# A new issue order in causal dilated attention and the recurrence beside it: key and query projections moved ahead, scores ahead of the turn

## The chip, the cores and the metric

The kernel is one program on one core of a Trainium2 chip. The metric is the device time of one execution in microseconds (us); lower is better. A core has a tensor engine (PE, with its weight loads shown apart as PEld), a vector engine (DVE), a scalar engine (ACT), a GpSimd engine (POOL) and a sync engine (SP) that here only issues DMAs. Each engine runs its own instructions strictly in the order in which they are written, and they meet at semaphores.

## What is computed

One decoder layer over 1024 tokens of width 1024, all in float32:

```
xn = rmsnorm(x); q, k, v, u = split(xn @ w_in)             # 4 x 512 columns
y_a = dilated causal attention(q, k, v) with T5 bias        # 8 heads of 64, three (window, dilation) patterns
y_b = S5(u): 32 groups, 64 complex states each, linear recurrence along the sequence, then GELU and a gate
h = x + [rmsnorm(y_a); rmsnorm(y_b)] @ w_out
h = h + cross attention(h, 256 memory rows)                 # its keys and values are projected early
h = h + mixture of experts(h): 4 of 32, 1024 wide, clamped SwiGLU
out = rmsnorm(h)
```

The three patterns of the dilated attention are handled as one softmax whose bias holds the logarithm of how many patterns include a distance, and minus 1e30 where none does.

## The kernel before

The program is five phases with a barrier of all engines after each. The change is wholly in the first, `phase_abc`: the projections, the set-up of the recurrence, the recurrence itself and the self attention. The later phases (the recurrence's output, the output projection, cross attention, the experts, the last norm) start when all engines have ended the first.

**Two rings of PSUM banks.** Transposes and small products go through `put` (L771), which uses banks 0 to 3 in turn: the product for place g waits until what place g-4 holds has been copied out. The list `plan(...)` (L317 to L344) says in which order the places come and whether ACT or DVE copies each. The wide projections go through `project` (L787), with banks 4 to 7 in turn; one projection product is eight 128-deep matmuls of up to 512 columns. The products are numbered: U (0 to 7), the memory keys (8 to 11), the memory values (12, 13), K (14 to 21), Q (22 to 29), V (30 to 37). The numbers, banks and weights of these are not changed. The weights of the six projections alternate between two buffers of 2 MB, `wa0` and `wa1`: U in 0, memory keys in 1, memory values in 0, K in 1, Q in 0, V in 1.

**The order on PE (L806 to L891).** The three small products for the attention's bias line (L814, one-hot rows times `rel_bias`); x transposed for the first half and U of it; x for the second half and the other U products; transposes for the recurrence's parameters; memory rows transposed, memory keys, memory values; then PE waits for `bt_ok` and `cp_step` 27, which say that the tables `BT` (built by POOL, L1084 to L1088) and `Cp` (built by DVE in `cp_of`, L626, nine steps of three operations over 128x512) are ready; then come the mixer's first products: transposes of `BT` (L855) and products with `U`, whose results DVE and ACT copy into `V`; the products that give `Krow`; the K projection; the products with `M1` (L884); the Q projection; the V projection; and last the attention. POOL starts the recurrence (L1098 to L1107, 128 steps of four dependent operations on `V`) when all of `V` is there. `M1` comes from `Krow` by way of a write to memory and eight loads by SP.

**The order on DVE (L634 to L707).** DVE copies the bias line, scales half of x's transposes, evicts the U products, then does `cp_of(0)`, the memory transposes, and for each memory key product one `cp_of`, the eviction, and one more `cp_of`; then its share of `V`, the K evictions, the `M1` results (32 operations), and the Q evictions.

**The order on SP (L387 to L468).** One queue: it loads the x rows and parameters; with U's products done it loads the weights of unit 2, writes `uT` to memory, waits for that write, issues the eight loads of `U`, and only then waits for the memory keys and loads the K weights, then the Q weights. Later come `Krow` out, `M1` in, the bias tiles 0 and 1, the V weights, and at the end bias tiles 2 and 3.

**The attention (L710 to L765, L893 to L967, L545 to L582).** There are 32 tiles t, each two heads and one block b of 128 queries (b runs from 0 to 7 inside each of four head pairs). For each tile there are these steps:

- `scores(t)` on PE: the near part (L900) and for b of 2 or more the far part (L906), into one of two pairs of banks;
- `maxima(t)` on DVE (L720): adds the bias, negates, and gives the row's extreme, for two heads;
- `exps(t)` on ACT (L557): exponentials and their sums;
- `divide(t)` on DVE (L727, L731): reciprocals of the sums, and the probabilities scaled by them;
- `turn(t)` on PE: transposes of the probabilities, near part (L917) into bank 4 and far part (L925) into bank 5;
- `near(t)` on ACT (L568) and `far(t)` on DVE (L745, L748): copies out of these two banks;
- `values(t)` on PE (L936), and at the end of a head pair `far_values` (L950), the squares on ACT (L573) and `out_of` on DVE (L755).

What the order of issue is, engine by engine, for each t:

```
PE :  turn(t)       scores(t+2)   values(t-1)   [far_values]
DVE:  maxima(t+1)   divide(t)     far(t)        [out_of]
ACT:  exps(t+1)     near(t)                     [squares_of]
```

Of the kernel before, what the change touches and what calls it, by code (L numbers as in the profile page):

```python
# [31 lines left out]
H_A, HD_A = 8, 64  # L32
# [8 lines left out]
T = 8  # L41
J = S // T
# [248 lines left out]
def phase_abc(nc, block, m, a, sem):  # L291
# [23 lines left out]
    banks, at = [], {}  # L315

    def plan(name, who):  # L317
        at[name] = len(banks)
        banks.append(who)

    for n in range(3):
        plan(("line", n), "dve")
    for half in range(2):
        for k in range(KC):
            plan(("x", half, k), "act" if k % 2 == 0 else "dve")
        plan(("rsb", half), "dve")
    plan("prm", "act")
    plan(("c", 0), "act")
# [17 lines left out]
    def t_bank(g):  # L346
        return m.ps[:, g % 4, :]
# [237 lines left out]
    def _(dve):  # L585
        def line_out_(n):
            g = at[("line", n)]
            dve.wait_ge(t_full, g + 1)
            lo, hi = 512 * n, min(512 * n + 512, LINE)
            nc.vector.tensor_copy(m.line[:, lo:hi], t_bank(g)[0:H_A, 0:hi - lo]).then_inc(t_dve, 1)  # L590
# [44 lines left out]
        nc.vector.memset(m.ztile[:], 0.0).then_inc(zero_ok, 1)  # L635
        for n in range(3):
            line_out_(n)
        dve.wait_ge(mix_in, 16)
# [4 lines left out]
        rsb_out(0)  # L643
        u_out_(0)
        for k in range(1, KC, 2):
            x_out(1, k)
# [13 lines left out]
        u_out_(7)  # L660
        cp_of(0)
        dve.wait_ge(gain_in, 16 * 14)
# [4 lines left out]
        for c in range(H_X):  # L667
            i = KM0 + c
            cp_of(1 + 2 * c)
            dve.wait_ge(p_full, i + 1)  # L670
            nc.vector.tensor_copy(m.kmT[:, c, :], p_bank(i)[:, 0:N_MEM]).then_inc(p_dve, 1)
            cp_of(2 + 2 * c)
        for q in range(8):
            g = at[("v", 1, q)]
            dve.wait_ge(t_full, g + 1)
            nc.vector.tensor_copy(m.V[:, 1:J + 1, 1, 4 * q:4 * q + 4], t_bank(g).rearrange("p (g j) -> p j g", g=4)).then_inc(t_dve, 1)

        def head_out(i, dst, s):
# [8 lines left out]
        for n in range(8):  # L687
            c, half = divmod(n, 2)
            head_out(K0 + n, m.kT[:, c, half * 512:(half + 1) * 512], None)
        for q in range(8):  # L690
            g = at[("y", q)]
            dve.wait_ge(t_full, g + 1)
            for n in range(4):
                w = 4 * q + n
                last = nc.vector.scalar_tensor_tensor(out=m.U[:, w, :], in0=m.U[:, w, :], scalar=m.dskip[:, w:w + 1],
                                                      in1=t_bank(g)[:, n * P:(n + 1) * P], op0=ALU.mult, op1=ALU.add)
            last.then_inc(t_dve, 1)
        dve.wait_ge(k_out, 16)
        for n in range(8):
            c, half = divmod(n, 2)  # L700
            head_out(Q0 + n, m.qT[:, c, half * 512:(half + 1) * 512], HD_A ** -0.5)

# [55 lines left out]
        for t in range(N):  # L758
            if t + 1 < N:
                maxima(t + 1)  # L760
            divide(t)
            far(t)
            if t % NB == 0 and t:
                out_of(t // NB - 1)
        out_of(3)  # L765

    @block.tensor
    def _(pe):
        group, product = [0], [0]

        def put(emit):  # L771

            g = group[0]
            if g >= 4:
                t_copied(pe, g - 4)
            emit(t_bank(g)).then_inc(t_full, 1)
            group[0] += 1
# [31 lines left out]

        pe.wait_ge(ones_row, 1)  # L810
        pe.wait_ge(oh_in, 32)
        for n in range(3):
            lo, hi = 512 * n, min(512 * n + 512, LINE)
            put(lambda out: nc.tensor.matmul(out[0:H_A, 0:hi - lo], m.rb[:], m.ohb[:, lo:hi], start=True, stop=True))  # L814
        pe.wait_ge(ident_ok, 3)
# [3 lines left out]
        for k in (6, 7):  # L819
            t_copied(pe, at[("x", 0, k)])  # L820
        by_weights(0, 0, 0)
        x_in_(1)
        by_weights(0, 1, 0)
# [33 lines left out]
        def four(operand, width=P):  # L857
# [5 lines left out]
            put(emit)  # L863

        pe.wait_ge(bt_ok, 1)
        pe.wait_ge(cp_step, 27)
# [9 lines left out]
        for q in range(8):  # L876
            four(lambda n: (m.BT[:, 4 * q + n, P - CH:P], m.Cp[:, 4 * q + n, 0:P]), CH)
        pe.wait_ge(wa_in[3], 16)
        for c in range(4):
            for half in range(2):  # L880
                by_weights(3, c, half)
        pe.wait_ge(m1_in, 16 * T)
        for q in range(8):
            four(lambda n: (m.M1[:, 4 * q + n, :], m.U[:, 4 * q + n, :]))  # L884
        pe.wait_ge(wa_in[4], 16)
        for c in range(4):
            for half in range(2):
                by_weights(4, c, half)
        pe.wait_ge(wa_in[5], 16)
        for b in range(NB):  # L890
# [66 lines left out]
        for i in range(V0 + 4, PROJECTED):  # L957
            p_copied(pe, i)
        for t in range(N + 1):
            if t < N:  # L960
                turn(t)
            if t + 2 < N:
                scores(t + 2)
            if t:
                values(t - 1)
                if t % NB == 0:
                    far_values(t // NB - 1)  # L967
# [1514 lines left out]
```

## Time and profile before

| what | us |
|---|---|
| median of 3 runs | 2673.07 (2672.39 to 2673.39) |
| the profiled execution, its own time | 2668.99 |
| its span in the profile | 2667.3 |
| 84 to 142, from the memory transposes to the mixer's first products | 58 |
| 342 to 494, the attention | 152 |
| 494 to 2667, the later phases | 2173 |

Times in the profile count from the start of the span. "PE busy" counts a pipelined matmul from its start to its modelled end, so the start of one group to the start of the next is the better measure of what it occupies. "idle before" is the time for which the engine did nothing ahead of that instruction, and the arrow names who released it. SPq is SP issuing a DMA: its length is that of the issue, not of the transfer. PEclk is the granted clock of PE, 1.00 for 2.4 GHz and 0.50 for 1.2 GHz.

### The profile page before, as it was taken

The numbers are of one execution on the slowest core, as the hardware profiler recorded it, in microseconds if no ns is written. First come the engines' busy times: TensorE is split into PE (matmuls) and PEld (weight loads), VectorE is DVE, ScalarE is ACT, GpSimd is POOL, SyncE is SP. The second block draws the span as 40 slices with busy tenths as digits, with TensorE's granted clock in tenths as the row PEclk, the third lists the DMA queues.
The fourth block names the chain that finished last, engine by engine and source line by source line (L and its number), as shares of the span: only waits on it lengthen the run. The fifth ranks groups of instructions, "written<-read, shape, count | busy, mean of one in ns | idle before, by whom it ended". The sixth has DMA issues, their size and how long they took to land. (4 is left out here: it accounts for less than half of the span.)

```text
span 2667.3 us, 29283 instructions
## 1 busy us (share of the span) xinstructions
PE 2454.2 (92%) x11352; PEld 1616.8 (61%) x11353; DVE 649.9 (24%) x1537; ACT 367.8 (14%) x824; POOL 422.4 (16%) x992
## 2 busy tenths in 40 slices
PE   8799966899989669999999999999999999999993
PEld 4465434645444257778696696786786786684441
DVE  2522044322243621112121221221221221221111
ACT  3020033201132000101101011011011111011101
POOL 3858810001001010000001001001000001001002
PEclk9899977898999889999999999999999999999996
DMA  8641000520001646776878878878888888889854
GB/s 191 136 66 38 24 15 1 161 77 32 0 1 58 254 143 191 229 244 217 260 253 267 274 252 268 280 261 259 277 270 263 294 285 281 294 291 304 287 181 142
DMA packets 373344, 508.04 MB, mean 190 GB/s; under 512 B 49031, under 2 KB 234631, under 8 KB 373204
## 3 DMA queue, kind: packets, MB, share of 16 engines
q1 hardware_dynamic: 360872, 469.43, 53.6%
q0 software_dynamic: 11008, 35.89, 6.0%
q8 instruction: 91, 1.49, 0.2%
q10 hardware_dynamic: 1324, 0.83, 0.1%
q14 instruction: 49, 0.40, 0.0%
HBM read 469.39 MB, written 38.77 MB: 191 GB/s over the span
## 5 line engine op out<-in xcount | busy, mean ns | idle before, releaser
L2055 PE MATMUL ps<-xT,we 128*128 128x160 f32 (+9 forms) x3584 | 516.4, 307 | 1.4 <-ACT xT L2302 1.4
L2055 PEld LDWEIGHTS ps<-xT,we 128*128 128x128 f32 x3584 | 508.3, 190 | 15.0 <-issue 8.0
L1997 PE MATMUL ps<-we,xT 128*128 128x512 f32 x1152 | 506.8, 594 | 0.0
L1997 PEld LDWEIGHTS ps<-we,xT 128*128 128x128 f32 x1152 | 213.8, 190 | 258.6 <-issue 258.6
L2069 PE MATMUL ps<-actT,we 128*128 128x160 f32 (+9 forms) x1792 | 261.1, 307 | 0.0
L2069 PEld LDWEIGHTS ps<-actT,we 128*128 128x128 f32 x1792 | 253.4, 190 | 5.6 <-DVE outT L2216 2.1
L2021 PE MATMUL ps<-we,actT 128*128 128x512 f32 x576 | 255.1, 596 | 0.7 <-ACT actT L2333 0.7
L1892 POOL DMA_INDIRECT acc_dram<-orow,sx x46 | 70.9, 1542 | 781.0 <-ACT orow L2313 488.2
L2325 ACT ACTIVATE sg<-glu 128x512 f32<-128x512 f32 (+9 forms) x92 | 49.8, 541 | 1041.1 <-DVE glu L2171 550.2
L2021 PEld LDWEIGHTS ps<-we,actT 128*128 128x128 f32 x576 | 106.5, 190 | 135.1 <-issue 134.2
L793 PE MATMUL ps<-xnT,wa 128*128 128x512 f32 x384 | 165.9, 592 | 0.0
L2190 DVE TENSOR_SCALAR glu<-ps,b1s 128x160 f32<-128x160 f32 (+9 forms) x112 | 44.0, 393 | 497.9 <-PE ps L2055 497.9
L1880 POOL DMA_INDIRECT xg<-xn_dram,gx x46 | 50.7, 1101 | 594.1 <-PE ps L1956 585.2
L793 PEld LDWEIGHTS ps<-xnT,wa 128*128 128x128 f32 x384 | 72.6, 190 | 90.1 <-issue 90.1
L286 POOL TENSOR_SCALAR ss<-ss 128x1 f32<-128x1 f32 (+1 forms) x36 | 7.9, 220 | 524.9 <-DVE ss L1315 171.6
L2171 DVE TENSOR_SCALAR glu<-ps 128x512 f32<-128x512 f32 x36 | 24.9, 692 | 270.0 <-PE ps L1997 270.0
L2216 DVE TENSOR_SCALAR outT<-ps,b2s 128x160 f32<-128x160 f32 (+9 forms) x112 | 44.0, 393 | 189.1 <-PE ps L2069 188.7
L1956 PE MATMUL ps<-ident,xg 128*128 128x128 f32 x368 | 56.5, 285 | 31.8 <-DMA xg<-xn_dram,gx 19.7
L2173 DVE TENSOR_SCALAR lin<-ps 128x512 f32<-128x512 f32 x36 | 24.9, 692 | 239.5 <-PE ps L1997 239.5
L2154 DVE TENSOR_SCALAR xT<-ps,g_moe 128x128 f32<-128x128 f32 (+9 forms) x184 | 46.6, 317 | 138.3 <-PE ps L1956 138.3
L917 PE MATMUL ps<-ident,pr 128*128 128x128 f32 x120 | 24.9, 339 | 51.4 <-DVE pr L731 51.4
L1956 PEld LDWEIGHTS ps<-ident,xg 128*128 128x128 f32 x368 | 42.1, 144 | 43.0 <-issue 27.2
(331 smaller groups left out, 2303.3 us busy)
## 6 DMA issues: line engine op xcount, KB each, us to landing
we<-in_w SPq DMA_DIRECT2D x384, 1024.0 KB, 6.3
wa<-in_w_in SPq DMA_DIRECT2D x4, 2048.0 KB, 8.5
xrow<-in_x SPq DMA_DIRECT2D x32, 128.0 KB, 6.7
wa<-in_w_xkv SPq DMA_DIRECT2D x2, 2048.0 KB, 9.7
h<-in_x SPq DMA_DIRECT2D x4, 1024.0 KB, 18.5
acc_dram<-h SPq DMA_DIRECT2D x1, 4096.0 KB
fin<-acc_dram SPq DMA_DIRECT2D x8, 512.0 KB, 8.8
out<-fout SPq DMA_DIRECT2D x32, 128.0 KB, 2.4
```

Of the source, the lines that this page charges most:

```text
L793: last = nc.tensor.matmul(p_bank(i)[:, 0:width], weights(k), moving(k), start=(k == 0), stop=(k == KC - 1))
L1880: pool.indirect_dma_start(xg[q % 2][0:rows, :], None, a.xn_dram, bass.IndirectOffsetOnAxis(m.gx[0:rows, s % 3, half:half + 1], 0), bounds_ ...
L1892: pool.indirect_dma_start(a.acc_dram, bass.IndirectOffsetOnAxis(m.sx[0:rows, s % 3, half:half + 1], 0), orow[q % 2][0:rows, :], None, boun ...
L1956: last = nc.tensor.transpose(out[:, P * i:P * i + P], xg[q % 2][:, k * P:(k + 1) * P], m.ident[:])
L1997: last = nc.tensor.matmul(m.ps[:, 2 * part + c, :], m.xT[:, 4 * half + k, 0:P], view[:, k, :], start=False, stop=(half == 1 and k == 3), s ...
L2021: last = nc.tensor.matmul(m.ps[:, 4 + n, :], m.actT[:, 4 * half + k, 0:P], view[:, k, :], start=False, stop=(half == 1 and k == 3), skip_g ...
L2055: last = nc.tensor.matmul(bank[:, part * WIN:part * WIN + W], view[:, k, (j % 2) * P:(j % 2 + 1) * P], m.xT[:, k, 0:W], start=(k == 0), st ...
L2069: last = nc.tensor.matmul(m.ps[:, 4 + j % 2, 0:W], view[:, k, (j % 2) * P:(j % 2 + 1) * P], m.actT[:, k, 0:W], start=(k == 0), stop=(k == ...
L2154: last = v.tensor_scalar(m.xT[:, i, half * P:half * P + cols], t_bank(g)[:, P * i:P * i + cols], m.g_moe[:, i:i + 1], None, ALU.mult)
L2190: v.tensor_scalar(m.glu[:, b, i * WIN:i * WIN + C], bank[:, 0:C], m.b1s[:, col, j:j + 1], LIMIT, ALU.add, ALU.min).then_inc(glu_ok, 1)
L2216: v.tensor_scalar(m.outT[:, j, 0:C], m.ps[:, 4 + j % 2, 0:C], m.b2s[:, col, j:j + 1], None, ALU.add).then_inc(l2_dve, 1)
L2325: nc.scalar.activation(dst, src, ACT.Sigmoid, scale=ALPHA).then_inc(swished, 1)
```

## The change

In the bank plan and on PE and DVE the bias line's three products and their copies come after the first U product instead of first. DVE does `cp_of` in nine places after the K evictions instead of before and among the memory keys' ones. On PE the K projection comes before the wait for the tables, and the Q projection before the products with `M1`; DVE's evictions follow that order. In the attention, PE issues `scores(t+2)` ahead of `turn(t)`, and DVE issues `far(t-1)` after `divide(t)` where it had issued `far(t)`. SP, ACT and POOL have the code they had; no operation is added or removed.

```diff
-    for n in range(3):
-        plan(("line", n), "dve")
     for half in range(2):
         for k in range(KC):
             plan(("x", half, k), "act" if k % 2 == 0 else "dve")
         plan(("rsb", half), "dve")
+        if half == 0:
+            for n in range(3):
+                plan(("line", n), "dve")
...
 DVE:
-        for n in range(3):
-            line_out_(n)
...
         rsb_out(0)
         u_out_(0)
+        for n in range(3):
+            line_out_(n)
...
         u_out_(7)
-        cp_of(0)
...
         for c in range(H_X):
             i = KM0 + c
-            cp_of(1 + 2 * c)
             dve.wait_ge(p_full, i + 1)
             nc.vector.tensor_copy(m.kmT[:, c, :], p_bank(i)[:, 0:N_MEM]).then_inc(p_dve, 1)
-            cp_of(2 + 2 * c)
...
             head_out(K0 + n, m.kT[:, c, half * 512:(half + 1) * 512], None)
+            cp_of(n)
+        cp_of(8)
+        (the eight copies into V, moved here from before the K evictions)
+        dve.wait_ge(k_out, 16)
+        (the eight Q evictions, moved here from behind the M1 results)
...
             if t + 1 < N:
                 maxima(t + 1)
             divide(t)
-            far(t)
+            if t:
+                far(t - 1)
             if t % NB == 0 and t:
                 out_of(t // NB - 1)
+        far(N - 1)
         out_of(3)
...
 PE:
         by_weights(0, 0, 0)
+        (the three line products, moved here from the start)
         x_in_(1)
...
+        pe.wait_ge(wa_in[3], 16)
+        for c in range(4):
+            for half in range(2):
+                by_weights(3, c, half)
         pe.wait_ge(bt_ok, 1)
         pe.wait_ge(cp_step, 27)
         bm_in(0)
...
         for q in range(8):
             four(lambda n: (m.BT[:, 4 * q + n, P - CH:P], m.Cp[:, 4 * q + n, 0:P]), CH)
-        (unit 3, the K projection)
-        (the products with M1)
         pe.wait_ge(wa_in[4], 16)
         for c in range(4):
             for half in range(2):
                 by_weights(4, c, half)
+        (the products with M1)
...
         for t in range(N + 1):
+            if t + 2 < N:
+                scores(t + 2)
             if t < N:
                 turn(t)
-            if t + 2 < N:
-                scores(t + 2)
             if t:
                 values(t - 1)
```

## Rows read from the trace of the kernel before

**Rows 1.** Busy time by stretch: length, engines, granted clock, DMA share, GB/s

```profile
84.00:142.00 58.00, 35.86 (x126) 24.36 (x125) 42.77 (x37) 4.72 (x10) 50.92 (x45) 0.82 0.75 181
342.00:494.00 152.00, 98.70 (x1120) 64.22 (x1120) 72.14 (x265) 61.05 (x168) 5.76 (x19) 0.81 0.04 7
494.00:2667.00 2173.00, 2048.50 (x9220) 1386.76 (x9220) 488.17 (x1134) 258.24 (x569) 179.54 (x314) 0.97 0.67 219
```

**Rows 2.** Waits, 342 to 494: us in total, times, longest

```profile
PE ps L917 <- DVE pr L731: 51.4, 32, 4.2
DVE prF L745 <- PE ps L925: 31.3, 24, 2.1
DVE sc L720 <- PE ps L906: 27.4, 21, 2.8
DVE yaT L755 <- ACT sqa L573: 18.3, 4, 5.0
```

**Rows 3.** Waits of PE from 60 to 345

```profile
PE ps L783 <- DVE memT L666: 12.2, 1, 12.2
PE ps L855 <- POOLq L1090: 9.2, 1, 9.2
```

**Rows 4.** The start: the bias line's products, from the timeline (start, us, engine)

```profile
6.22 4.42 PE L814 MATMUL ps<-ohb,rb 33*8 33x512 f32 x6 [6.22 <-DMA rb<-in_rel_bias]
```

**Rows 5.** Timeline, 84 to 142, of PE, DVE and SP

```profile
93.40 0.69 DVE L630 TENSOR_TENSOR tmp<-CrCi,F 128x512 f32<-128x512 f32 x1 [8.50 <-POOLq L1067]
98.14 8.25 SPq L428 DMA_DIRECT2D U<-u_dram  x8
99.76 16.25 PE L793 MATMUL ps<-memT,wa 128*128 128x256 f32 x64 [0.63 <-ACT memT L517]
115.85 13.90 PE L793 MATMUL ps<-wa,memT 128*128 128x512 f32 x32
116.05 0.39 SPq L385 DMA_DIRECT2D wa<-in_w_in  x1
```

**Rows 6.** DMA issues, 60 to 200: KB each, median us to landing

```profile
wa<-in_w_in SPq DMA_DIRECT2D x2, 2048.0 KB, 7.8
U<-u_dram SPq DMA_DIRECT2D x8, 256.0 KB, 10.2
```

**Rows 7.** The DMA engines while U loads (columns of Rows 1)

```profile
112.00:114.00 2.00, 2.00 (x11) 1.77 (x10) 2.00 (x2) 0.00 (x0) 1.84 (x3) 1.00 1.25 124
```

**Rows 8.** Timeline of one tile of the attention, full clock

```profile
399.24 0.65 PE L917 MATMUL ps<-ident,pr 128*128 128x128 f32 x4 [1.45 <-DVE pr L731]
400.04 0.70 PE L900 MATMUL ps<-kT,qT 64*128 64x256 f32 x4
401.11 0.66 PE L936 MATMUL ps<-prT,v 128*64 128x128 f32 x8
401.28 0.59 DVE L720 CUSTOM_DVE_ANT_0 sc<-ps,bias 128x416 f32<-128x416 f32 x1 [0.71 <-PE ps L906]
402.50 0.75 DVE L731 TENSOR_SCALAR pr<-pr,den 128x384 f32<-128x384 f32 x2
403.31 0.66 PE L917 MATMUL ps<-ident,pr 128*128 128x128 f32 x4 [1.55 <-DVE pr L731]
404.22 0.42 DVE L745 COPY prF<-ps 128x256 f32<-128x256 f32 x1 [0.97 <-PE ps L925]
```

**Rows 9.** Timeline of PE in a tile at half clock

```profile
348.48 1.12 PE L917 MATMUL ps<-ident,pr 128*128 128x128 f32 x4 [2.13 <-DVE pr L731]
352.97 1.11 PE L917 MATMUL ps<-ident,pr 128*128 128x128 f32 x4 [1.21 <-DVE pr L731]
354.44 1.23 PE L900 MATMUL ps<-kT,qT 64*128 64x256 f32 x4
356.10 0.98 PE L936 MATMUL ps<-prT,v 128*64 128x128 f32 x8
```

**Rows 10.** The recurrence's first and last step, and divisions beside and after it

```profile
161.06 0.46 POOL L1102 TENSOR_TENSOR scan_t<-V,a 128x128 f32<-128x128 f32 x1 [22.04 <-DVE V L676]
347.41 1.01 DVE L731 TENSOR_SCALAR pr<-pr,den 128x256 f32<-128x256 f32 x2
348.56 0.25 POOL L1107 TENSOR_TENSOR V<-V,scan_t 128x32 f32<-128x32 f32 x1
385.01 0.62 DVE L731 TENSOR_SCALAR pr<-pr,den 128x256 f32<-128x256 f32 x2
```

More of the change, by code:

```diff
@@ L668, in _ @@
             i = KM0 + c
-            cp_of(1 + 2 * c)
             dve.wait_ge(p_full, i + 1)
             nc.vector.tensor_copy(m.kmT[:, c, :], p_bank(i)[:, 0:N_MEM]).then_inc(p_dve, 1)
-            cp_of(2 + 2 * c)
[L673 to L676, printed above, removed]
         def head_out(i, dst, s):
@@ L689, in _ @@
             head_out(K0 + n, m.kT[:, c, half * 512:(half + 1) * 512], None)
+            cp_of(n)
+        cp_of(8)
+        for q in range(8):
+            g = at[("v", 1, q)]
+            dve.wait_ge(t_full, g + 1)
+            nc.vector.tensor_copy(m.V[:, 1:J + 1, 1, 4 * q:4 * q + 4], t_bank(g).rearrange("p (g j) -> p j g", g=4)).then_inc(t_dve, 1)
+        dve.wait_ge(k_out, 16)
+        for n in range(8):
+            c, half = divmod(n, 2)
+            head_out(Q0 + n, m.qT[:, c, half * 512:(half + 1) * 512], HD_A ** -0.5)
         for q in range(8):
@@ L697, in _ @@
             last.then_inc(t_dve, 1)
[L698 to L701, printed above, removed]
         nc.vector.memset(m.vfar[ST:P, 1], 0.0).then_inc(far_zero, 1)
@@ L808, in rsb_ @@
             put(lambda out: nc.tensor.matmul(out, m.ones[:], m.diag[:].rearrange("p n t -> p (n t)"), start=True, stop=True))
[L810 to L814, printed above, removed]
         pe.wait_ge(ident_ok, 3)
@@ L821, in _ @@
         by_weights(0, 0, 0)
+        pe.wait_ge(ones_row, 1)
+        pe.wait_ge(oh_in, 32)
+        for n in range(3):
+            lo, hi = 512 * n, min(512 * n + 512, LINE)
+            put(lambda out: nc.tensor.matmul(out[0:H_A, 0:hi - lo], m.rb[:], m.ohb[:, lo:hi], start=True, stop=True))
         x_in_(1)
@@ L877, in _ @@
             four(lambda n: (m.BT[:, 4 * q + n, P - CH:P], m.Cp[:, 4 * q + n, 0:P]), CH)
[L878 to L884, printed above, removed]
         pe.wait_ge(wa_in[4], 16)
@@ L888, in _ @@
                 by_weights(4, c, half)
+        pe.wait_ge(m1_in, 16 * T)
+        for q in range(8):
+            four(lambda n: (m.M1[:, 4 * q + n, :], m.U[:, 4 * q + n, :]))
         pe.wait_ge(wa_in[5], 16)
```

## The prediction

> **What bounds the kernel now.** I read the busy time by stretch first. The change is all in the first phase, which ends just before 494 us with a barrier; the 2173 us behind it hold none of the edited code, and all of it starts when the first phase ends, so it should only move [rows 1]. In the first phase two stretches are not full. From 84 to 142 PE is busy for 35.9 of 58 us, and in the attention (342 to 494) for 98.7 of 152, with no engine above 72% and PE at 0.81 of its clock on average [rows 1]. That is a chain from engine to engine, not an engine's own work, so the waits come next. PE waited once for 12.2 us for memT's eviction by DVE, and once for 9.2 us ahead of the mixer's first product [rows 3]. In the attention PE waits 51.4 us for the divided probabilities; DVE waits 31.3 us for the far transposes, 27.4 us for the scores and 18.3 us for the squares at the four ends of a head pair [rows 2]. DVE's three waits (77 us) and its 72.1 us of work fill the stretch.
>
> The loop is seen in one tile at full clock: turn starts at 399.24, scores at 400.04, values at 401.11; DVE's maxima start at 401.28, the divisions at 402.50, and the next turn at 403.31 [rows 8]. The period is 4.07 us: turn 0.80, scores 1.07, a hop of 0.17, maxima 1.2, division 0.8. Each of these waits for the one before, since PE puts scores(t+2) behind turn(t), and DVE puts divide(t+1) behind maxima(t+2), which needs those scores.
>
> **Part 1, the bias line's products.** They ran in 4.42 us, six instructions at half the pace (0.74 each, against 13.90/32 = 0.43 us for 512 columns at full clock [rows 5]), in time that PE spends waiting for x anyway [rows 4]. Behind the first U product PE is full: they cost 2 x 0.43 + 2 x 0.43 + 2 x 0.22 = 2.2 us. Their three copies on DVE fit beside this but push x's second half by about as much. SP's write of the line comes late in its queue, and its wait is met long before. Cost: +2.1 us. Ends: 0 if the second half of x is the later one anyway, +4.4 if they run at the pace of [rows 4].
>
> **Part 2, DVE no longer holds memT.** cp_of(0) waited until 93.4 for POOL's tables with memT's evictions queued behind it [rows 5]. Now they follow the U evictions at once. The wait of 12.2 goes [rows 3], and some 0.4 us at its edge: -12.6. What was late next were the memory keys: 64 instructions of 256 columns took 16.25 us, at 0.22 each they are 13.9 [rows 5]; the difference is the half clock after the idle time (granted clock 0.82 in this stretch [rows 1]). With PE not stopped this goes too: -2.3. The memory values ended at 115.85 + 13.90 = 129.75 [rows 5] and would end at 129.75 + 2.1 - 12.6 - 2.3 = 117.0.
>
> **Part 3, the K projection next, and its weights.** This is the new wait. SP's order is not changed: it issues the U loads, and then the K weights. The U loads were issued from 98.14 for 8.25 us [rows 5], after the write of uT, whose start follows U's last product (+2.1): so the K weights are issued at 98.14 + 8.25 + 2.1 = 108.5, not at 116.05. In the trace they land in 7.8 us (median of two) when nothing is beside them [rows 6]; but at 108.5 the DMA engines are full of U's small pieces (share 1.25 for 124 GB/s [rows 7]; landing 10.2 us [rows 6]). No load of 2 MB beside these is in the trace. Ends: 108.5 + 8 = 116.5, no wait; or one after the other, U ending at about 115.5 + 2.1 and the weights 7 us behind, 124.2. I take 124.2, for the DMA engines have no free share: +7.2, and +2.4 for restarting at half clock, as measured on the memory keys. Worst end: 130. The Trainium skill (DMA: Bandwidth & Descriptors, section Queues, rings and completion order) says that descriptors of one issuing engine's rings are consumed in ring order; by that the weights stand behind U, as I take it, and the no-wait end would be out.
>
> **Part 4, the tables.** The old 9.2 us wait goes: BT needs POOL until about 140 at worst, and K now ends near 124.2 + 2.4 + 55.6 = 182 (8 products of 16 instructions of 0.434). In its place DVE holds PE: cp_of(7) and cp_of(8) stand behind the last K eviction, so seven operations of 0.69 (the only one of them that ran with POOL idle in between [rows 5]) and a hop: +5.0. Net -4.2. Ends: -9 if the steps were done early (they can't be), -2 if they take twice as long each. The mixer's first products, Krow's, M1's and the V projection keep their lengths. The chain from Krow to M1 was hidden by the K projection and is now hidden by the Q projection, which is as long; SP then has Q's 55 us and M1's products to issue the bias tiles and V's weights.
>
> Sum up to the attention: +2.1 - 12.6 - 2.3 + 7.2 + 2.4 + 5.0 - 9.2 = **-7.4 us**. Ends: -17 (no wait for the weights) and -1.
>
> **Part 5, the attention's order.** PE has scores(t+2) done before it waits for divide(t), so the loop through the scores spans two tiles, and DVE never waits for its own turn: far(t-1) was transposed a tile ago. DVE's waits for scores and far transposes, 27.4 + 31.3, go [rows 2]. 152 - 58.7 = 93; each DVE step still has a hop of 0.05, some 90 of them: 97 us if nothing else binds. That is for one tile like the one shown: maxima 1.05, reciprocal and divisions 0.95, far 0.42 [rows 8], 2.5 us where it was 4.07. PE's own tile at full clock is 0.80 + 1.07 + about 0.45 = 2.3, just under it. The two-tile loop is turn 0.8 + values 0.45 + scores 1.07 + hops 0.3 + maxima 1.05 + division 0.95 = 4.6, 2.3 a tile. The 18.3 us at the ends of head pairs stay: values, far values, squares and out_of still come one after the other.
>
> Two things take from this. First PE's clock. A mean of 0.81 in 152 us is (1 - 0.81) x 2 x 152 = 58 us at half clock [rows 1]. There PE needs 1.47 for the turn, 1.66 for the scores [rows 9], about 0.9 for the values: 4.0 us, more than DVE's 2.5; the old period there was 352.97 - 348.48 = 4.5. By the granted clock of 2 us windows it fell after the idle time at the start and at the ends of head pairs, which stay, and inside two of the pairs, where PE will be fuller. I take 40 us at half clock: 40 x (1 - 2.6/4.0) = 14. Ends: none, and the whole stretch (32 tiles at 4.0, less for the short first blocks, and the pair ends: about 147 us). Second, the recurrence. It took 348.8 - 161.1 = 187.7 us [rows 10] and started when V was there; K is now ahead of that, so it starts near 182 + 5 + 21 = 208 and ends near 396, while the attention starts at 334.6. For 61 us the divisions share with POOL: beside the recurrence a pair over 256 columns took 1.01 us, after it 0.62 [rows 10]. +0.25 to +0.4 for each of some 20 tiles: +6. Ends: 0 (hidden where PE binds) and +8. With 4 us for hops that I can't place, the attention takes 97 + 14 + 6 + 4 = 121 us: **-31 us**, about. Ends: 100 and 147.
>
> The Trainium skill (SBUF — State Buffer, section SBUF: two separate sides) speaks against this overlap: DVE in a two-port mode and GpSimd exclude each other for a whole instruction. The rows above agree. By the rule alone POOL could lose at each division too, by at most their 0.8 us a tile.
>
> **Sum.** Profiled execution: 2669.0 - 7.4 - 31 = 2630.6. It ran 4.1 us below the median of the runs, so I predict 2673.1 - 38.4 = 2634.7, rounded to **2635 us**. A change of 0.2% is 5.3 us, about what can be told from none.
>
> **Rivals.** (a) PE keeps its full clock and DVE is the bound: the attention takes 102 us and 6 for the sharing, -44, and half of the wait for the weights is gone, -10 ahead of it: **2619 us**. For it: PE would be 90% busy in a tile. Against: the idle time at pair ends stays, and the clock fell there. (b) The loop closes again at another place: turn's far part needs bank 5, which far(t-1) empties only after divide(t) now, and DVE's maxima wait for nothing less; or PE stays at half clock. Then a tile takes 4.0 and the attention some 140 us: -11 - 7 = **2655 us**. For it: PE at half clock alone gives 4.0. Against: far takes 0.42 while the near transposes take 0.5. (c) The other side: the recurrence becomes the end of the phase. It starts 47 us later and the barrier waits for it. It decides if it ends after 456; it makes the kernel slower than before if it ends after 494. At 334 some 86 steps are done and 42 are left of 1.47 us each; they would have to take 3.8 us each. At 4.2 us a step it would end at 510 and the time would be **2689 us**. Against: a tile holds at most 0.8 us of divisions for about two steps. (d) The reorder doesn't do what it says, because DVE's divide(t) is late by the exponentials of ACT and not by the scores: ACT works 61 us of 152 [rows 1], exps(t) start a tile ahead, so I give it nothing of its own; it would look like (b) with **2665 us**.
>
> **Chances.** Forecast 0.60, with its own range 2622 to 2648; (a) 0.16; (b) 0.17, (d) 0.02; (c) 0.02; another place that I don't see, with no gain, 0.03. The range for 8 in 10 takes most of (a) and the nearer part of (b): 2618 to 2656. Faster by over 0.2%: 0.95; within: 0.02; slower: 0.03.
>
> **What would show it.** Right: no wait of PE at the memory transposes; one of about 7 us ahead of the first K product for DMA wa, and one of about 5 us ahead of L855 for DVE Cp; the last step of the recurrence near 400 us, inside the attention; DVE waits at L720 and L745 nearly gone and DVE near 75% busy until the pair's end; the attention near 121 us with a granted clock of 0.85 or more; the stretch after it unchanged at 2173. Wrong: a wait of turn for far or of scores for the maxima that takes the place of the old one, a clock near 0.5 through the attention, or a recurrence that ends after it.

## The result and the profile after

| what | before | after |
|---|---|---|
| median (4 runs each) | 2673.23 (2672.39 to 2675.05) | 2614.65 (2614.16 to 2616.54) |
| the profiled execution, its own time | 2668.99 | 2614.62 |
| its span | 2667.3 | 2612.9 |
| first maxima of the attention (start) | 342.12 | 333.80 |
| last `out_of` (end) | 492.96 | 436.33 |
| the attention between these two | 150.8 | 102.5 |

The change makes the kernel 58.6 us faster; the ratio of the times is 0.9781, with a 95% interval of 0.9764 to 0.9798. The forecast was 2635, 20 us too slow, and the measured time lies 3 us under the range. The two profiled executions differ by 54.4 us, since the one of before ran 4 us below its median: 8.3 us are gained ahead of the attention and 48.3 in it, and 2.2 are lost behind it (2173.2 and 2175.4 us for the later phases; in the twelve further profiles they took between 2172.4 and 2175.7, whatever the kernel, so I read that as noise).

Busy time by stretch of the kernel after (columns as in [rows 1]): 84 to 142, the attention with a little on either side, and the later phases.

```profile
84.00:142.00 58.00, 50.05 (x155) 28.50 (x155) 7.81 (x16) 2.99 (x6) 44.30 (x52) 0.94 0.74 182
332.00:437.00 105.00, 85.83 (x1120) 57.87 (x1120) 73.35 (x267) 59.99 (x169) 55.29 (x174) 0.90 0.07 11
437.40:2612.90 2175.50, 2050.13 (x9220) 1388.15 (x9220) 488.03 (x1134) 258.19 (x569) 179.54 (x314) 0.97 0.67 219
```

PE now works 50.1 of the 58 us where it worked 35.9, and the same 1120 matmuls and about the same 72 us of DVE's work fit into 105 us instead of 152.

**Ahead of the attention.** PE's waits from 60 to 330 us, kernel after. The 12.2 and 9.2 us of [rows 3] are gone, and the two foretold waits stand in their place.

```profile
PE ps L795 <- DMA wa<-in_w_in: 7.3, 1, 7.3
PE ps L857 <- issue: 4.9, 1, 4.9
PE ps L795 <- ACT memT L518: 0.6, 1, 0.6
```

Lines from the timeline of PE and SP there, to set beside [rows 4, 5], kernel after (L795 is a projection; 124.84 is the first K product):

```profile
30.06 2.31 PE L823 MATMUL ps<-ohb,rb 33*8 33x512 f32 x6
86.82 2.28 PE L785 MATMUL ps<-ident,memrow 128*128 128x128 f32 x16
89.73 14.05 PE L795 MATMUL ps<-memT,wa 128*128 128x256 f32 x64 [0.62 <-ACT memT L518]
101.64 7.82 SPq L429 DMA_DIRECT2D U<-u_dram  x8
103.61 13.90 PE L795 MATMUL ps<-wa,memT 128*128 128x512 f32 x32
109.50 8.43 SPq L386 DMA_DIRECT2D wa<-in_w_in  x2
124.84 6.54 PE L795 MATMUL ps<-xnT,wa 128*128 128x512 f32 x10 [7.33 <-DMA wa<-in_w_in]
186.90 1.94 PE L857 MATMUL ps<-ident,BT 128*128 128x128 f32 x8 [4.88 <-issue]
```

The memory transposes run in one piece and start 2.9 us later than before (83.95 then, behind the line products). The memory keys take 14.05 us instead of 16.25. The values end at 117.5, the K weights were issued at 109.50 and let PE go at 124.84. The wait ahead of L857 names only "issue"; DVE's timeline shows what it was, the table `Cp` finished at 186.80, 0.1 us before PE goes on:

```profile
182.13 0.69 DVE L676 TENSOR_TENSOR kT<-ps,rsb 128x512 f32<-128x512 f32 x1 [4.25 <-PE ps L795]
186.11 0.69 DVE L633 TENSOR_TENSOR Cp<-tmp 128x512 f32<-128x512 f32 x1
```

**In the attention.** The waits from 332 to 437 us, kernel after (total, times, longest), against [rows 2]:

```profile
ACT prT L569 <- PE ps L919: 27.1, 32, 1.6
DVE yaT L755 <- ACT sqa L574: 16.2, 4, 4.4
PE ps L919 <- DVE pr L731: 13.5, 9, 3.5
DVE sc L720 <- PE ps L908: 12.4, 14, 1.7
```

DVE's wait for the far transposes fell from 31.3 to 0.8 us, the one for the scores from 27.4 to 12.4, PE's for the probabilities from 51.4 to 13.5. One tile at full clock, to set beside [rows 8]:

```profile
400.48 0.56 PE L908 MATMUL ps<-kT,qT 64*32 64x192 f32 x16
400.97 0.66 PE L919 MATMUL ps<-ident,pr 128*128 128x128 f32 x4
401.15 0.62 DVE L720 CUSTOM_DVE_ANT_0 sc<-ps,bias 128x448 f32<-128x448 f32 x1 [0.21 <-PE ps L908]
401.77 0.66 PE L938 MATMUL ps<-prT,v 128*64 128x128 f32 x8
402.44 0.79 DVE L731 TENSOR_SCALAR pr<-pr,den 128x416 f32<-128x416 f32 x2
403.14 0.42 DVE L745 COPY prF<-ps 128x256 f32<-128x256 f32 x1
403.28 0.66 PE L919 MATMUL ps<-ident,pr 128*128 128x128 f32 x4 [0.42 <-DVE pr L731]
```

From turn to turn it is 2.3 us here, and 2.51 us for the tile that took 4.07 before. The maxima wait only 0.21 us for scores, and `far` follows the divisions at once, for the turn before.

### The profile page after: what moved, and what is told of

Same layout as the page of the kernel before. It is cut to its first block and busy times, and to the rows that moved or that the text cites. A ratio compares the mean times of both kernels' runs of the same rounds, so it can differ in the third digit from the quotient of the medians.

```text
span 2612.9 us, 29286 instructions
## 1 busy us (share of the span) xinstructions
PE 2439.1 (93%) x11352; PEld 1609.2 (62%) x11353; DVE 627.9 (24%) x1537; ACT 365.7 (14%) x824; POOL 415.6 (16%) x992
## 5 line engine op out<-in xcount | busy, mean ns | idle before, releaser
L2057 PEld LDWEIGHTS ps<-xT,we 128*128 128x128 f32 x3584 | 508.8, 191 | 15.3 <-issue 8.0
L795 PE MATMUL ps<-xnT,wa 128*128 128x512 f32 x384 | 168.0, 598 | 7.3 <-DMA wa<-in_w_in 7.3
L795 PEld LDWEIGHTS ps<-xnT,wa 128*128 128x128 f32 x384 | 73.4, 192 | 99.5 <-issue 91.3
L2173 DVE TENSOR_SCALAR glu<-ps 128x512 f32<-128x512 f32 x36 | 24.9, 692 | 269.7 <-PE ps L1999 269.7
L2175 DVE TENSOR_SCALAR lin<-ps 128x512 f32<-128x512 f32 x36 | 24.9, 691 | 239.9 <-PE ps L1999 239.9
L1104 POOL TENSOR_TENSOR scan_t<-V,a 128x128 f32<-128x128 f32 x128 | 58.5, 457 | 30.6 <-DVE V L688 20.7
```

The lines of the kernel that those rows point to most:

```text
L795: last = nc.tensor.matmul(p_bank(i)[:, 0:width], weights(k), moving(k), start=(k == 0), stop=(k == KC - 1))
L1104: tt(m.scan_t[:], now.unsqueeze(1).to_broadcast([P, 2, 2, G]), a8, ALU.mult).then_inc(scan_step, 1)
L2057: last = nc.tensor.matmul(bank[:, part * WIN:part * WIN + W], view[:, k, (j % 2) * P:(j % 2 + 1) * P], m.xT[:, k, 0:W], start=(k == 0), st ...
```

## The experiments

Each kernel is compared with the kernel before, run on the same chip beside it. The first four split the change, the next four each touch one of its terms, and the last four ask what the terms are worth together.

### The two attention orders, one by one and together

The first kernel has only the new order on PE, the second only the one on DVE, the third both; the projections and tables of all three are as in the kernel before.

```diff
 PE (first and third):
         for t in range(N + 1):
+            if t + 2 < N:
+                scores(t + 2)
             if t < N:
                 turn(t)
-            if t + 2 < N:
-                scores(t + 2)
 DVE (second and third):
-            far(t)
+            if t:
+                far(t - 1)
...
+        far(N - 1)
```

> The kernel before with PE's new order in the attention alone (scores(t+2) ahead of turn(t)); DVE still issues far(t) right behind divide(t), and the first 340 us are as before. Theory A, one loop: DVE must still sit out its own turn, so a tile is divide 0.95, turn 0.8 and a hop, far 0.42, maxima 1.05, in all 3.5 us in place of 4.07 at full clock: attention 150.8 less 15 to 22, about 132 us. The wait of DVE for the far transposes stays near 25 us and the one for the scores nearly goes. Rival B, each wait is worth its length: the 27.4 us of waiting for scores goes and nothing else, 123 us. Rival C, the gain came from PE's clock: the clock in the attention rises to 0.9 here as well, and half clock falls from 58 us to about 20.

> The kernel before with DVE's new order in the attention alone (far(t-1) behind divide(t)). Theory A: the loop turn, scores, maxima, divide is untouched, since PE still puts the scores behind the turn and the far copy was beside the scores anyway: attention 150.8 within 4 us; DVE's wait for far goes and its wait for the scores grows by as much. Rival B, each wait is worth its length: 31.3 us less, 120 us. Rival C, clock: granted clock as before, 0.81, no change.

> The kernel before with both new orders in the attention and nothing else. Theory A: attention 101 to 103 us as in the changed kernel, less about 2 us for the recurrence that is no longer beside it: 150.8 - 49 to 51, time before less 49 to 51. More than the sum of the two single edits by 25 us or more. Rival B: the sum of the two single edits. Rival D, part of the gain belongs to the new place of the projections (PE comes into the attention with another history): attention 108 us or more here.

The kernel before ran at 2671.68 beside them (19 runs). Attention is from the first maxima to the end of the last `out_of`.

| kernel | median us | ratio [95%] | attention us | granted clock |
|---|---|---|---|---|
| scores ahead of turn only | 2641.3 | 0.9887 [0.9869, 0.9906] | 120.6 | 0.90 |
| far(t-1) only | 2671.19 | 0.9997 [0.9988, 1.0007] | 153.7 | 0.77 |
| both | 2619.84 | 0.9803 [0.9786, 0.9819] | 102.6 | 0.88 |

DVE's waits in the attention with PE's order alone:

```profile
DVE prF L745 <- PE ps L925: 33.3, 24, 3.4
DVE yaT L755 <- ACT sqa L573: 15.7, 4, 4.1
DVE sc L720 <- PE ps L906: 0.7, 1, 0.7
```

and with DVE's order alone:

```profile
DVE sc L720 <- PE ps L908: 51.3, 21, 3.4
DVE yaT L755 <- ACT sqa L573: 18.1, 4, 6.1
DVE prF L745 <- PE ps L927: 2.3, 2, 1.5
```

Each order removes its own one of the two waits of [rows 2]. PE's order removes that for scores (27.4 to 0.7) and leaves that for the far transposes, and gains 30.2 us of attention. DVE's order removes that for the far transposes (31.3 to 2.3), and the same time comes back as more waiting for scores (27.4 to 51.3): it gains nothing that can be told (0.5 us in the medians). Alone it only moves the wait along one loop, for scores(t+2) are still issued behind turn(t). Once PE's order has opened that loop, the same edit is worth 120.6 - 102.6 = 18 us. The third kernel has the attention of the full change (102.6 and 102.5 us), without any of its edits ahead of it.

The granted clock differs between these kernels (0.81 before), so the attention's length alone does not tell the order's own part. One tile at full clock does: the time from the divisions of block 4 to those of block 5, from DVE's timelines. In each kernel it is the same within 0.01 us in every head pair in which it ran at full clock.

| kernel | us |
|---|---|
| before | 4.04 |
| scores ahead of turn only | 3.24 |
| far(t-1) only | 4.04 |
| both, and the full change | 2.52 |

At an equal clock, then, PE's order takes 0.80 us off a tile, DVE's order alone nothing, and both together 1.52.

Against what was expected: PE's order had been put at about 132 us of attention and 3.5 us a tile; it took 120.6 and 3.24, and the time at half clock fell with it from 58 to 24 us, as its third rival had said. DVE's order came out as expected. The two together gained 21 us more than the single edits added up, where 25 or more had been expected.

### The placements alone

The full change with the attention's two old orders: the reverse of the diff above, on the kernel after.

> The changed kernel with the old orders in the attention: only the projections, cp_of and the bias line's products moved. Theory A: 8.3 us less than before up to the attention, and the attention slower by 1 to 3 us where the divisions are beside the recurrence (to about 398 us): 5 to 8 us less than before in all. Rival D: 10 us or more less, the attention gaining from the placement.

It ran at 2668.05, ratio 0.9986 [0.9977, 0.9996]: 3.6 us faster. The first maxima start at 333.7, 8.4 us earlier than before, but the attention takes 153.4 us, 2.6 more. The recurrence now runs beside it, and its divisions total 23.5 us against 22.5. So of the front's gain a part is given back with the old orders (the medians gained 3.6, where 5 to 8 had been expected); with the new orders it is kept. Whether the longer divisions are the cause is not shown: this profile also had 61 us of its attention at half clock, where the kernel before had 58. The two halves of the change add up, 51.8 + 3.6 against 58.6 (56.8 in a later repeat), to within what these runs can tell.

### The bias line's products at the start again

The full change, with the three products and their copies ahead of everything as before.

```diff
-        (behind the first U product)
+        (ahead of x_in_(0))
         for n in range(3):
             lo, hi = 512 * n, min(512 * n + 512, LINE)
             put(lambda out: nc.tensor.matmul(out[0:H_A, 0:hi - lo], m.rb[:], m.ohb[:, lo:hi], start=True, stop=True))
```

> The changed kernel with the bias line's three products and copies back at the start. Theory A: PE's second half of x starts 2.2 us earlier, and DVE's copies are out of the way of x's second half as well; in the changed kernel the memory transposes start at 86.82 and before at 83.95, so 2.9 us less all through (the K weights, whose issue hangs on U's last product, come with it). Rival: the wait for the K weights takes it up, since the write and reload of U sets when they are issued: K's first product stays at 124.8 and the time is the same within 1 us.

It ran at 2611.18 beside 2670.44 for the kernel before (9 runs), ratio 0.9774 [0.9760, 0.9787]. The memory transposes start at 84.07 instead of 86.82: the move had cost 2.75 us there. The first K product, however, waits 8.00 us for its weights instead of 7.33 and starts only 2.1 us earlier, and the first maxima only 0.9 us. The rest went into the half clock behind the two waits: the 128 K matmuls took 57.9 us (57.2 in the kernel after) and the first sixteen products with `U` 3.0 (2.6). How long PE stays slow behind a wait differs from run to run, by about as much as this edit is worth there. So the expected 2.9 us did not come; the 0.9 us is the rival's number (the same within 1 us) but not for its reason, since K did start earlier.

### The K weights ahead of the loads of U

```diff
         sp.wait_ge(u_out, 16)
+        sp.wait_ge(p_full, VM0)
+        weights_in(3)
         for s in range(T):
             (the loads of U)
-        sp.wait_ge(p_full, VM0)
-        weights_in(3)
```

> The changed kernel with SP issuing the K weights ahead of the eight loads of U (both behind the write of uT and the memory keys). Theory A: issued at 104, they have the DMA engines to themselves and land near 112; the wait of 7.3 us ahead of K's first product goes, K starts at 117.5 at full clock, and 9 to 10 us go in all; the U loads end some 2 us later, far ahead of their use near 180. Rival: the engines serve both at once; the weights land after 117.5 and 3 us or less go.

It ran at 2604.93, ratio 0.9748 [0.9735, 0.9762]. The timeline of SP and PE of this kernel:

```profile
103.11 0.37 SPq L386 DMA_DIRECT2D wa<-in_w_in  x1
103.52 13.57 SPq L431 DMA_DIRECT2D U<-u_dram  x8
102.85 13.90 PE L795 MATMUL ps<-wa,memT 128*128 128x512 f32 x32
116.58 55.10 PE L795 MATMUL ps<-xnT,wa 128*128 128x512 f32 x128
```

The weights are issued 6.4 us earlier than in the kernel after, and PE does not wait for them at all: K starts at 116.6 instead of 124.8. Its 128 matmuls take 55.1 us; behind the wait they took 57.2 in the kernel after. So the wait cost its own 7.3 us and 2.1 for the restart at half clock. The first maxima start 9.3 us earlier, and the attention ends 8.5 us earlier, where 9 to 10 in all had been expected. The loads of U, pushed back to 103.5, delay nothing, because their first use stands behind the whole K projection now.

The two traces together also show how the loads shared the queue. Columns as in [rows 1], with the rate in GB/s last, in stretches of 2 us; first in the kernel after:

```profile
108.00:110.00 2.00, 2.00 (x6) 0.86 (x5) 0.00 (x0) 0.00 (x0) 1.84 (x3) 1.00 1.24 129
112.00:114.00 2.00, 2.00 (x6) 0.84 (x5) 0.00 (x0) 0.00 (x0) 1.92 (x2) 1.00 1.25 129
120.00:122.00 2.00, 0.00 (x0) 0.00 (x0) 0.00 (x0) 0.00 (x0) 1.84 (x3) 1.00 1.05 410
```

and then in this one:

```profile
106.00:108.00 2.00, 2.00 (x7) 0.81 (x6) 0.00 (x0) 0.00 (x0) 1.84 (x3) 1.00 1.05 410
114.00:116.00 2.00, 2.00 (x6) 0.95 (x5) 0.00 (x0) 0.00 (x0) 1.84 (x3) 1.00 1.23 124
```

In the kernel after the rate stays at that of U's small pieces for 8 us after the weights are issued at 109.50, and then rises to 410 GB/s; the weights land 15.3 us after their issue. In this kernel the 410 come first and the small pieces behind; the weights land after 8.2 us, though U's loads stand right behind them. One load ran after the other, in the order of issue, both times.

### The last tables earlier

```diff
             head_out(K0 + n, m.kT[:, c, half * 512:(half + 1) * 512], None)
-            cp_of(n)
-        cp_of(8)
+            if n < 4:
+                cp_of(2 * n)
+                cp_of(2 * n + 1)
+            elif n == 4:
+                cp_of(8)
```

> The changed kernel with cp_of two at a time behind each of the first four K evictions and the last one behind the fifth. Theory A: DVE has 6 us free behind each eviction and a pair takes 4.1; all nine are done 20 us ahead of the wait; PE's 4.9 us ahead of the mixer's first products go, and about 1 us more because PE doesn't restart there after idle time: 5 to 6 us less. Rival: DVE evicts K later, or shares with POOL's last steps of BT (until 130), and the wait is only moved: 2 us or less.

It ran at 2605.76, ratio 0.9753 [0.9740, 0.9767]. PE does not wait ahead of the mixer's first products any more. The first maxima start 6.6 us earlier, which is 1.7 more than the wait's 4.9: the granted clock was 0.67 in the 5.1 us behind that wait in the kernel after, and 1.00 there in this one. The attention ends 5.4 us earlier, as expected.

### The clock held at the ends of head pairs

At the end of a head pair PE stands still for 3.5 us and runs at half clock afterwards. The timeline of PE at the end of the second pair, kernel after:

```profile
384.61 0.70 PE L902 MATMUL ps<-kT,qT 64*128 64x256 f32 x4
385.24 0.34 PE L908 MATMUL ps<-kT,qT 64*32 64x64 f32 x16
389.06 1.11 PE L919 MATMUL ps<-ident,pr 128*128 128x128 f32 x4 [3.48 <-DVE pr L731]
```

The experiment puts 14 products, whose result nobody reads, into that idle time, at the start of pairs 2, 3 and 4 (the profile counts two matmul records for each).

```diff
             b = tiles[t][1]
+            if b == 1 and t > 1:
+                for i in range(14):
+                    nc.tensor.matmul(m.ps[:, 5, 0:P], m.ident[:], m.ident[:], start=True, stop=True)
             pe.wait_ge(divided, 2 * t + 2)
```

> The changed kernel with 14 useless products of 128 columns into bank 5 (free there) ahead of the turn of the second tile of head pairs 2, 3 and 4, which fill PE's idle time of 3.3 us at a pair's end. Theory A: PE keeps its full clock there; of the 20.5 us at half clock in the attention some 13 go, and tiles of 3.3 to 3.7 us become 2.5 to 2.9: attention 102.5 less 2 to 4 us. Rival, the price of the prediction (35% of the time at half clock): 5 us or more. Rival: nothing, since the pair's first tiles wait for DVE.

It ran at 2604.29, ratio 0.9751 [0.9737, 0.9764]. The same place in its timeline; the turn takes 0.66 us again:

```profile
381.05 3.39 PE L915 MATMUL ps<-ident 128*128 128x128 f32 x28
384.46 0.66 PE L922 MATMUL ps<-ident,pr 128*128 128x128 f32 x4
```

and its attention by stretch, at full clock from end to end and 94.0 us long:

```profile
334.00:428.00 94.00, 87.40 (x1204) 62.62 (x1204) 72.01 (x264) 58.76 (x168) 54.58 (x170) 1.00 0.07 11
```

So half the clock cost 102.5 - 94.0 = 8.6 us (before rounding) in the kernel after. Only 2 to 4 us had been expected of this edit; the rival, 5 us or more, was right. But not all of that is due to the added products. The first pair has none, and it was at full clock in this profile and at half clock from 336 to 343 in the kernel after. That differs from run to run, as the last section shows by pairs.

### The change again, the front mended, and both

The front mended has the three edits ahead of the attention together (line products first, K weights ahead of U, tables early); the next kernel has the held clock too.

> The changed kernel itself once more, as the reference for the runs of this call: 57 to 60 us below the kernel before.

> The changed kernel with the three mends of its own new costs together: bias line's products first, K weights ahead of the U loads, cp_of two at a time. Theory A: each stands on a place of its own; the attention ends 8.5 + 5.3 us sooner for the two waits and 2.8 us for the line, which no wait takes up any more: at about 419.7 in place of 436.3, 16 to 17 us less than the changed kernel. Rival: without the idle time between them the K evictions and cp_of meet POOL's BT steps (K starts at 115, BT ends near 128), a wait comes back, and 12 us or less go.

> The same with the 14 useless products at the pair ends. Theory A: 8 us more go, about 25 us less than the changed kernel in all, the attention taking 94 us. Rival: the clock falls elsewhere in turn (at the start of the attention or in a pair), and 4 us or less go.

Beside them the kernel before ran at 2672.21 (9 runs, 2669.00 to 2674.27).

| kernel | median us (5 runs) | ratio [95%] |
|---|---|---|
| the change again | 2615.42 | 0.9786 [0.9772, 0.9799] |
| front mended | 2594.38 | 0.9711 [0.9698, 0.9725] |
| front mended, clock held | 2589.25 | 0.9694 [0.9681, 0.9707] |

The three mended edits are worth 21.0 us together and move the first maxima from 334.9 to 314.9. Singly they had moved them from 333.8 by 0.9, 9.3 and 6.6, which is 16.8, and 16 to 17 us had been expected of the three. With no wait behind them the line products' 2.75 us are gained in full (+1.8), and this run of the changed kernel started the attention 1.1 us later than the first, with its granted clock at 0.50 instead of 0.67 behind the wait for the tables: 19.7 of the 20.0. The held clock is worth 5.1 us more, where 8 had been expected. The last version is the fastest here, 26.2 us below the changed kernel and 83 below the kernel before.

### The held clock without the recurrence

The kernel with the clock held, and only 1 of the 128 steps of the recurrence; the other 127 are left out.

```diff
-        for j in range(J):
+        for j in range(1):
```

> The changed kernel with the clock held, and with only one of the 128 steps of the recurrence done (the rest of it is left out), to price the sharing of DVE and POOL at full clock. The attention took 93.9 us with the recurrence beside its first 64 us. Theory A: divisions were 2 us longer in sum and DVE is the bound, so 91.5 to 92.5. Rival, the price of the prediction: 88. Rival, hidden: 93.9, the same.

One run, 2610.19 us, its attention 96.8 us: longer, not shorter, than with the recurrence, and outside all that was expected. By pairs the reason is seen. Each number is the time from one `out_of` (L755) to the next, the first one from the first maxima, all read from DVE's timelines.

| kernel | pair 1 | pair 2 | pair 3 | pair 4 |
|---|---|---|---|---|
| after | 27.08 | 25.04 | 26.14 | 22.86 |
| the change again | 26.58 | 26.21 | 26.64 | 22.88 |
| clock held | 24.07 | 23.52 | 23.58 | 21.38 |
| clock held, no recurrence | 27.37 | 23.32 | 23.31 | 21.38 |
| front mended | 26.17 | 26.03 | 26.42 | 22.83 |
| front mended, clock held | 27.07 | 23.57 | 23.51 | 21.38 |

Pair 1 takes 24.1 us at full clock and 26.2 to 27.4 where its first tiles ran at half; of these six it ran at full clock in one. That one is the profile of the clock-held kernel, which makes its 94.0 us some 3 us better than it was made by the edit. Pairs 2 to 4 hold the answers. The added products shorten them from 75.3 to 68.5 us (front mended, without and with), or 6.8 us where the medians differ by 5.1. And the recurrence beside them costs 0.20 and 0.27 us in pairs 2 and 3 at full clock, and nothing in pair 4, which it does not reach. The groups of DVE from the end of one `out_of` to another over these two pairs show where its price went, first with the recurrence:

```profile
L720 DVE CUSTOM_DVE_ANT_0 sc<-ps,bias 128x288 f32<-128x288 f32 (+7 forms) x32 | 14.5, 489 | 1.5 <-PE ps L908 1.4
L731 DVE TENSOR_SCALAR pr<-pr,den 128x256 f32<-128x256 f32 (+7 forms) x32 | 13.2, 454 | 0.6
```

and without it:

```profile
L720 DVE CUSTOM_DVE_ANT_0 sc<-ps,bias 128x288 f32<-128x288 f32 (+7 forms) x33 | 15.0, 490 | 2.9 <-PE ps L908 2.7
L731 DVE TENSOR_SCALAR pr<-pr,den 128x256 f32<-128x256 f32 (+7 forms) x32 | 11.0, 386 | 0.6
```

The divisions are 2.2 us longer beside POOL (454 against 386 ns each), but DVE then waits 1.3 us less for scores and 0.4 less for the squares: a tile is bound by PE as much as by DVE here, and what one loses is taken out of its wait for the other.

## Why the prediction was right in kind and too small in size

The forecast had the mechanism and the sign, and every step showed up where it was foretold. What failed is the size of the attention's term: 121 us forecast, 102.5 measured. The difference of 18.5 us is nearly the whole error of 20. The forecast's own lower end for the attention, 100 us, had held the measured value; the range drawn from it, from 2618, did not.

**Ahead of the attention: right.** -7.4 forecast, -8.3 measured. The line products cost 2.9 at the memory transposes (2.1 forecast). The wait for memT went and the memory keys took 14.05 us, as forecast. The wait for the K weights, taken as 7.2, was 7.3, with 2.1 for the restart (2.4 forecast); the wait for the last tables, taken as 5.0, was 4.9. That the DMA engines had no share left for a load beside U's pieces was the right reading of [rows 7]: the K weights, issued at 109.50, landed at 124.8, though 7.8 us is what such a load took with nothing beside it [rows 6]. That the wait came out to 0.1 us is in part luck: U's last piece landed at 119.9 and not at 117.6, and the weights 4.9 us behind it and not 7. The Trainium skill (DMA: Bandwidth & Descriptors, section Queues, rings and completion order) says that each DMA engine consumes its descriptors in ring order; the rates of both orders, shown with the experiment on the K weights, agree with it. Engines shared evenly would have moved both loads at once, at a rate in between, and no stretch shows that for longer than the change from one load to the other. What the forecast left out is that PE also restarted more cheaply behind the tables. It ran at half clock behind the old 9.2 us wait too, for 6.3 us, and behind the new one for 3.4: from the first transposes of `BT` to the next projection it took 28.3 us before and 26.9 after. These 1.4 us outweigh the line's 0.8 and account for the -8.3 to within 0.3.

**Attention, the loop: right.** Both waits of DVE, 58.7 us, were said to go; 13.2 are left (12.4 and 0.8), and with the clock held 4.3 (3.5 and 0.8). A tile of 2.5 us was forecast, and 2.51 measured.

**Attention, the base: 97 against 94.0.** With the clock held, 94 us hold 72.0 us of DVE's work, as before, and 16.1 us of waits for squares, 4.3 for scores and far transposes, and about 1.5 of other gaps. The forecast had 18.3 for the squares and 4 to 5 for hops of 0.05; the hops are mostly not there.

**The sharing with the recurrence, +6: this step failed.** The divisions did become longer beside POOL, by 2.4 us in sum (22.5 before, 24.9 after), not by 6. The 1.01 us of [rows 10] is one pair of divisions, taken as the price of each, and over two pairs the mean is 454 ns for one beside it and 386 without: 0.14 us a tile, where 0.25 to 0.4 was forecast. Even that did not pass to the end: 0.2 to 0.3 us a pair. The recurrence lost little too: 187.7 us before, 189.7 with 64 us of it beside the attention. And the kernel with both orders alone, whose recurrence ended 7 us into the attention, had the same attention of 102.6 us. The rule of the Trainium skill (SBUF — State Buffer, section SBUF: two separate sides) has the two engines exclude each other for a whole instruction when DVE works in a two-port mode; the longer divisions agree with it (454 against 386 ns).

**The half clock, 14 us: this step failed too.** I took 40 us at half clock; 20.7 are in the trace. I had asked where the clock had fallen in the old trace, and left the falls inside the pairs half in place; with PE full inside the pairs none of them is left, only those at the starts of the four pairs. Their price per us was underrated: 8.6 us for 20.7, or 0.42, where I had 1 - 2.6/4.0 = 0.35 (block 3 of the third pair, all of it at half clock, took 3.72 us and at full clock 2.30). Twice the time at five sixths of the price gave 5.4 too much.

**"4 us for hops that I can't place": this step failed.** There were none. The four terms of the error are 3.0 for the base (it includes the sharing that is left), 6 for the sharing, 5.4 for the clock, 4 for the hops: 18.5 before rounding. All lay on one side, because each was a loss added for caution on top of a base that had already its margin. The gain of the attention was counted as the two waits less four allowances; the chain of the new order, 2.3 to 2.5 us a tile, was right by itself.

**The rivals.** (a), at 2619 the nearest, was right that DVE is close to full inside the pairs. Its 102 us agree with the measured 102.5 by two errors that cancel: it had no half clock, which cost 8.6, and a base 8 us above the one seen at full clock, 94.0. Its 6 us for the sharing came on top and are not there. (b), a loop that closes again at the far bank, is refuted: in the new order no wait of PE names `far`, and `far` itself waits 0.8 us. Its half clock held in no pair from end to end. (c) did not come near: the recurrence ended at 397.4, inside the attention, at 1.48 us a step. (d) is refuted by the same waits, as ACT's own work is the same and DVE's wait for it is only at the pair ends. The clock's own part in the gain was not measured by itself: the attention before had 58 us at half clock and the new one 20.7, and PE's order alone brought the 58 to 24, so most of that is an effect of the shorter waits. An estimate: in the kernel before, the tile of block 4 took 5.31 us wholly at half clock (third pair) and 3.89 at full, 0.27 per us; for 58 us that is about 15.5 us, against 8.6 in the new order. By this some 7 of the 48 us came through the clock and some 41 through the order at an equal clock.

## What to carry to other kernels

Where two engines serve each other in order, find the loop through both instruction streams and move in each the step whose input is a turn old; one of the two moves alone may be worth nothing (0.5 us here) or a part (30), and both 52. When a new order is priced, take the loop's own period and add only losses that have a count in the trace; an allowance for each thing that could go wrong put four on one side here. After work is moved forward, look at the queue that feeds it: SP's order, left as it was, cost 9 us of the 21 that three small edits gave back.

## What was not expected of the hardware

An idle time of 3.5 us of PE was followed by half clock each time, and 14 useless products in it kept the granted clock at 1.00 through the rest; they cost nothing that is seen, for from the first to the second divisions of these pairs it is 7.7 to 7.8 us with them and without. Whether the clock falls in the attention's first tiles differs between runs of kernels that are the same up to there, at a cost of 2 to 3 us, and so does the time at half clock behind the wait for the tables (0.67 and 0.50 in two runs of one kernel), so a single profile can be off by that much. The Trainium skill (TensorE: Matmul & The Clock Gate, section HAM oscillation — how this bites in real kernels) describes how PE, stalled by a wait for data, starts its next work at the low clock; these traces agree, at the pair ends and behind the two waits ahead of the attention. The later phases' 2172 to 2176 us did not follow any of this.
